# Low parts of the feed-forward weights: from VectorE's subtraction to a negated copy and an adding DMA

## What is computed

```python
for l in range(2):
    hn = rmsnorm(x, g_mix)
    u_a, u_b = split(hn @ w_in)                      # 1024 x 1024
    y_a, h_last = s5_mixer(u_a, h0, ...)             # complex-diagonal scan, GELU, half-GLU
    y_b, hist = pool_mixer(u_b, ...)                 # trailing windows 2, 4, 8, 16
    x = x + concat(y_a, y_b) @ w_out                 # 1024 x 1024
    hf = rmsnorm(x, g_ffn)
    x = x + square(relu(hf @ w_ff1)) @ w_ff2         # 1024 x 4096, 4096 x 1024
return rmsnorm(x, g_final), states, histories
```

## Time and profile before

| | |
|---|---|
| median of 3 runs | 2121.94 us (2121.08 to 2123.07) |
| profiled execution | 2121.07 us, its span 2119.1 us |
| TensorE, matmul | 2063.7 us busy (97%) |
| VectorE | 1070.9 us (51%) |
| ScalarE | 447.7 us (21%) |
| GpSimd | 214.1 us (10%) |
| mean granted clock of TensorE | 0.996 of full speed |
| DMA | 152.77 MB, mean 72 GB/s |

### The profile page before, as it was taken

One profiled execution on the slowest core, in us unless ns is written; L12 is line 12 of the kernel. 1 busy time (PEld: TensorE's weight loads), 2 busy tenths in 40 slices (PEclk: granted clock), 3 DMA queues, 4 the chain that ended last, 5 costly groups with the idle time before them and its releaser, 6 DMA issues.

```text
span 2119.1 us, 29080 instructions
## 1 busy us (share of the span) xinstructions
PE 2063.7 (97%) x12888; PEld 2030.9 (96%) x12888; DVE 1070.9 (51%) x1423; ACT 447.7 (21%) x560; POOL 214.1 (10%) x294
## 2 busy tenths in 40 slices
PE   8999899999999999999999999999999999999997
PEld 7888899999999999999999889999999999999997
DVE  7988464455453535353558725633343434333346
ACT  6232431111010111111332234311111111111112
POOL 2353120000000000010110331100000000000003
PEclk9999999999999999999999999999999999999999
DMA  5455111111211112123242641111111111111112
GB/s 177 135 150 161 53 55 51 46 44 41 92 60 52 60 42 70 42 65 129 95 139 64 196 115 41 40 50 40 50 40 41 50 41 50 41 50 41 45 46 85
DMA packets 62493, 152.77 MB, mean 72 GB/s; under 512 B 8576, under 2 KB 21408, under 8 KB 61984
## 3 DMA queue, kind: packets, MB, share of 16 engines
q1 hardware_dynamic: 49552, 112.76, 17.3%
q0 software_dynamic: 9072, 24.65, 4.2%
q10 hardware_dynamic: 3744, 13.50, 1.6%
HBM read 123.36 MB, written 27.53 MB: 71 GB/s over the span
## 4 chain that ended last, share of the span: by engine, by line
PE 94%; DVE 2%; ACT 2%; issue 1%; DMA 1%; POOL 0%; ACTq 0%; DVEq 0%; POOLq 0%
PE tile L509 89%; PE tile L827 2%; PE small L721 1%; PE small L715 1%; PE small L623 1%; PE small L597 0%; ACT w_high L861 0%; DMA y_a<-ya_dram 0%; DVE pool_s L1210 0%; POOL y_a L1841 0%; DMA ya_dram<-u_blocks 0%; PE small L565 0%; PE small L538 0%; DVE y_a L1665 0%; ACT u_blocks L1095 0%
## 5 line engine op out<-in xcount | busy, mean ns | idle before, releaser
L1548 DVE TENSOR_TENSOR x<-tile,x 128x816 f32<-128x816 f32 (+1 forms) x304 | 205.7, 719 | 490.8 <-PE tile L509 480.9
L509 PE MATMUL tile<-h_high,w_high 128*128 128x408 f32 (+1 forms) x1920 | 426.1, 330 | 10.6 <-DVE w_low L1223 10.6
L509 PE MATMUL tile<-h_low,w_high 128*128 128x408 f32 (+1 forms) x1920 | 422.7, 328 | 0.0
L509 PE MATMUL tile<-h_high,w_low 128*128 128x408 f32 (+1 forms) x1920 | 422.3, 328 | 0.0
L509 PEld LDWEIGHTS tile<-h_high,w_high 128*128 128x128 f32 x1920 | 320.5, 188 | 13.8 <-issue 12.4
L509 PEld LDWEIGHTS tile<-h_low,w_high 128*128 128x128 f32 x1920 | 320.2, 188 | 1.0
L509 PEld LDWEIGHTS tile<-h_high,w_low 128*128 128x128 f32 x1920 | 319.9, 188 | 1.0
L509 PE MATMUL tile<-hidden_high,w_high 128*128 128x408 f32 (+1 forms) x1440 | 317.9, 329 | 0.7
L509 PE MATMUL tile<-hidden_low,w_high 128*128 128x408 f32 (+1 forms) x1440 | 316.4, 328 | 0.0
L509 PE MATMUL tile<-hidden_high,w_low 128*128 128x408 f32 (+1 forms) x1440 | 316.3, 328 | 0.0
L861 ACT ACTIVATE w_high<-w_raw 128x1024 fp32r<-128x1024 f32 x162 | 170.6, 1053 | 664.1 <-PE tile L509 656.7
(11 more groups left out here) (212 smaller groups left out, 1687.0 us busy)
## 6 DMA issues: line engine op xcount, KB each, us to landing
w_raw<-w_blocks SPq DMA_DIRECT2D x164, 512.0 KB, 3.7
x<-x_t ACTq DMA_DIRECT2D x8, 544.0 KB, 10.8
u_blocks<-ua_dram SPq DMA_DIRECT2D x64, 68.0 KB, 2.8
ya_dram<-u_blocks ACTq DMA_DIRECT2D x8, 544.0 KB, 3.5
y_a<-ya_dram POOLq DMA_DIRECT2D x64, 68.0 KB, 2.7
x_kept<-x ACTq DMA_DIRECT2D x8, 544.0 KB, 2.7
cy_dram<-y_quarter POOLq DMA_DIRECT2D x16, 256.0 KB, 2.9
carry_weights<-cy_dram POOLq DMA_DIRECT2D x8, 512.0 KB, 5.2
```

Of the source, the lines that this page charges most:

```text
L509: mm = pe.matmul(ps[tile][:, c, 0:(b - a) * J], lhs, xt[:, k, a * J:b * J], start=(first and n == 0), stop=(last and n == 2))
L1548: ins = v.tensor_tensor(xt, pt_, xt, ALU.add)
```

## The change

For the 128 blocks of the two feed-forwards (`by_adders`), the low part is made in another way. ScalarE writes the high part as before and then, in a second pass over the raw block, minus the high part into the slot of the low part: a copy with scale -1, rounded by its output format as the first one is. GpSimd waits for it and issues a DMA from `raw` to `wlo` that adds to what is there. The 36 blocks of the mixers stay with VectorE. SyncE and TensorE wait for a low part by `low_ready`: for these blocks it is the landing of the DMA, one semaphore for each slot.

```diff
+        def by_adders(b):
+
+            return b < LAYERS * NB and b % NB >= B_FF
+
+        def low_ready(eng, b):
+
+            l, n = divmod(b, NB)
+            if by_adders(b):
+                eng.wait_ge(wlo_added[b % 2], 16 * (l * (NB - B_FF) // 2 + (n - B_FF) // 2 + 1))
+            else:
+                eng.wait_ge(wlo_made, l * B_FF + n + 1)
...
                 if b > 1:
-                    sp.wait_ge(wlo_made, b - 1)
+                    low_ready(sp, b - 2)
...
             def block_at(b):
-                pe.wait_ge(wlo_made, b + 1)
+                low_ready(pe, b)
...
                 act.activation(w_parts(b)[0], raw[:, b % 2, :], ACT.Copy).then_inc(whi_made, 1)
+                if by_adders(b):
+                    act.activation(w_parts(b)[1], raw[:, b % 2, :], ACT.Copy, scale=-1.0).then_inc(wneg_made, 1)
...
             def split_lo(b):
-                if b < LAYERS * NB:
+                if b < LAYERS * NB and not by_adders(b):
...
-            def add_squares(phase):
+            def add_squares(phase, blocks):
+
                 for m in range(1, KD):
...
+                    if m in blocks:
+                        add_low(blocks[m])
+
+            def add_low(b):
+
+                l, n = divmod(b, NB)
+                pool.wait_ge(wneg_made, l * (NB - B_FF) + n - B_FF + 1)
+                pool.dma_start(w_parts(b)[1], raw[:, b % 2, :], accum_op=ALU.add).then_inc(wlo_added[b % 2], 16)
+
+            def add_lows(l, after):
+
+                for n in range(2, 8 * NC - (2, 0)[l]):
+                    add_low(l * NB + B_FF + n)
+                    cc, n = divmod(n, 8)
+                    if l == 0:
+                        after(cc, n)
...
-            add_squares(1)
-            rotations_out()
-            for q in range(4):
-                drive_weights_out(q)
-                carry_weights_out(1, q)
-                kernels_out(1, q)
-            add_squares(2)
+            add_squares(1, {5: B_FF, 7: B_FF + 1})
+
+            def tables_out(cc, n):
+
+                if cc == 2 and n == 7:
+                    rotations_out()
+                if cc in PREP_CHUNKS and n == 5:
+                    drive_weights_out(PREP_CHUNKS[cc])
+                    carry_weights_out(1, PREP_CHUNKS[cc])
+                if cc - 1 in PREP_CHUNKS and n == 0:
+                    kernels_out(1, PREP_CHUNKS[cc - 1])
+            add_lows(0, tables_out)
+            add_squares(2, {1: NB - 2, 3: NB - 1})
...
-            add_squares(3)
+            add_squares(3, {5: NB + B_FF, 7: NB + B_FF + 1})
+            add_lows(1, None)
```

More of the change, by code:

```diff
@@ L255, in hybrid_trunk @@
         wlo_made = sem("wlo_made")
+        wneg_made = sem("wneg_made")
+        wlo_added = [sem(f"wlo_added{i}") for i in range(2)]
         tile_done = sem("tile_done")
```

## The result

| | before | after |
|---|---|---|
| median, same chip | 2122.11 us (2121.08 to 2123.07, 4 runs) | 2142.08 us (2141.02 to 2142.4, 4 runs) |
| profiled span | 2119.1 us | 2139.1 us |
| ratio | | 1.0096, 95% interval 1.0083 to 1.0109 |

The change makes the kernel 20 us slower, where 2143 was forecast. The page of the changed kernel, parts 1, 5 (count, busy us, mean ns, idle before it) and 6 (KB, median us to landing), answers to the earlier trace rows. VectorE's L1223 is now L1239, ScalarE's L861 is L875.

A forecast was written before the change was run, and what follows sets the result against it. TensorE, busy 97% of the span, was taken as the bound, with at most 1.5 us to win. Starts 9.0, half clock 4.8, end 7.5 and turn 0.5 made 21.8; 2121.1 + 21.8 = 2143 us, range 2131 to 2230.

The forecast's parts named there:

- the named places: Where little time is spare: start of each feed-forward, the program's end, the turn to layer 1; 21.8 us together.
- Rival 1: Steady feed-forward chunks stall because the add takes over 7.2 us: 2180 at 8 us, over 2400 at 13; chance 0.28.
- D: Time from when GpSimd's adding DMA may be issued until its data count as landed; taken as 5.5 us.
- Rival 2: Whole program not slower: loss under 4 us if the add lands within 2.6 us, 2124; chance 0.04.
- Rival 3: In layer 0, GpSimd's queue order or a rotations store delays adds at nine places, 2150 to 2161; chance 0.06.
- stops at the two starts, 2 x (D - 1.0): At each feed-forward's third block TensorE waits 4.5 us for the low part, 9.0 together.
- half clock behind them: After each stop at a feed-forward start TensorE runs at 1.2 GHz, losing 2.4 us, 4.8 together.
- the end: Low part of the block before the last two lands late: 6.5 us by data alone, 7.5 with the clock.
- the turn to layer 1: The add shares the engines with a store of x, with 6.1 us of room; 0.5 us lost.
- I keep the slower figure from the rows: Choosing 5.5 us for the add, from a store beside a fetch in the trace, over some 4.1.
- The estimate by the Trainium skill: Add at half a copy's rate, 2.1 us plus 2 us fixed, some 4.1; the sum would be about 12 us.
- 2D - 4.5: Delay of the program's end through the last block's data, fetched only after the preceding add lands; 6.5 us.

The follow-up runs named there:

- e1: Changed kernel with the third feed-forward block of each layer given back to VectorE: 2128.29 us, ratio 1.0035 to the kernel before.
- e2: Changed kernel with the last three blocks of the program given back to VectorE: 2134.39 us, ratio 1.0061 to the kernel before.
- e3: Changed kernel with six blocks back on VectorE (third of each feed-forward, third of layer 0's last chunk, last three): 2121.82 us, 1.0003.
- e7: Kernel before, plus minus passes and DMA adds into an unread buffer for 58 of layer 1's feed-forward blocks: 2121.57 us, 1.0001.
- e4: Changed kernel, TensorE running 21 discarded high-part products before waiting at each layer's third feed-forward block: 2138.73 us, ratio 1.0087.
- e6: Changed kernel with every DMA add done twice, the second issued after the first has landed: 2302.11 us, ratio 1.0845.
- e10: All 128 blocks by DMA add, products needing the low part taken last where TensorE stopped: 2128.8 us, ratio 1.0032.
- e8: Changed kernel, last three blocks on VectorE, low-part products taken last where TensorE stopped and at the very first product: 2120.63 us, 0.9995.
- e5: Changed kernel with GpSimd's DMA copying the raw block over the low part instead of adding: 2134.39 us, ratio 1.0057.

## Why the prediction was right

**Right in mechanism, by experiment.** The loss sits at the named places (e1, e2, e3), the 120 or so adds between them are free (e3, e7), and the clock's share is real (e4). TensorE had waited for VectorE for 1.5 us; taking VectorE's work away could win no more, and the longer way lost wherever less than its length was to spare. Rival 1 (steady stalls) needed D over 7.2 and got 4.4; e6 shows that it exists, with the edge where the prediction put it (7.5 with the hops, against 7.4). Rival 2 (not slower) needed D at 2.6: even a bare copy takes 2.9 and is 13 us slower than before. Rival 3 (GpSimd's order) shows nothing at D = 4.4, but the traffic of layer 1's tables does, with 0.35 us at 1003. Rival 1 was priced too low: for D = 9.3 the prediction has 2230, and e6, whose two adds take 9.3 us from the first issue to the second landing, took 2302. It left out most of the half clock behind so many stops and the longer adds of layer 0.

**Terms of the sum.**

| term | forecast | measured |
|---|---|---|
| D, issue to landing | 5.5 | 4.4, and 0.42 of hops that I left out |
| stops at the two starts, 2 x (D - 1.0) | 9.0 | 3.88 + 3.86 = 7.7 |
| half clock behind them | 4.8 | 2.3 + 1.5 = 3.8 |
| the end | 7.5 | 7.4 |
| the turn to layer 1 | 0.5 | 0.0 |
| other | 0 | 0.6 (layer 0's last chunk), 0.2 |

The step that was off is D: "I keep the slower figure from the rows". I took a plain store beside a fetch for the model, both transfers and all. The estimate by the Trainium skill (Collectives: The Full Stack, the bandwidth ceiling, with DMA: Bandwidth & Descriptors, anatomy of one DMA), 4.1, was nearer to 4.4. With 4.4 my formula gives 6.8 for the two stops; they were 7.7, since I left out the hops to GpSimd and back there, which I had counted in the budget. Two errors of opposite sign; the sum was 1.8 too high. The two starts together moved by 12.0, 0.5 more than their stops and clock. The rest is in the matmuls behind a stop: at full clock in e4 the 216 took 36.01, where the pace of the kernel before gives 35.76, 0.25 us at each start.

Three sums of the prediction are off without effect on its argument. For D = 4 it adds 11 us and writes 2131, where 2121.1 + 11 is 2132. For D = 7.2 its terms give about 2151, not 2155. And SyncE's fetch, by its own rows, starts 1.99 + 5.5 - 2.3 = 5.2 us later than before, not 4.3.

**The end came out by luck, in its size.** The 7.5 of the sum is TensorE's own path, 2078.3 - 2070.8: a restart 5.1 us later and 2.4 us of half clock. Measured were 4.6 and 2.8, two errors that cancel. The path through the last block's data, 2D - 4.5, was the earlier one by 1 us in the forecast (2077.3), and it was the earlier one in the run, by only 0.5 us: TensorE reached the seventh partial tile at 2090.92, and the last add landed 5.5 us after its issue, at 2090.4.

```profile
2084.89 0.86 POOL L1795 DMA_DIRECT2D w_low_last<-w_raw  x1 [8.70 <-ACT w_low_last L877]
...
2090.92 0.35 PE L841 MATMUL tile<-hidden_high,w_high_last 128*128 128x408 f32 x1
```

With D = 4.4 the formula for the data gives 4.3, but the last two adds took 5.7 and 5.5 us, and the fetch between them 4.5; why the last add was slow, with no other transfer beside it, the runs do not show. Without the 2.8 us of half clock TensorE would have waited for it for some 2.3 us (an estimate from these times). In e10, where TensorE stands less before it, the data are late. The clock's delay and the data's are not to be added; whichever is later counts.

## What to carry to other kernels

Moving work off an engine pays by what the bound engine waits for that engine, here 1.5 us of 2119, and costs wherever the new way is longer than the time to spare: look for the few places with the least room (starts of stages, the end), not at the mean. If a longer way is wanted all the same, let the consumer begin with what does not need it, as in e8, or leave those few blocks on the short way, as in e3. Price a stop of TensorE with its half clock too: here 1.3 to 2.8 us behind stops of 2.3 to 6 us, and no half clock behind two of 2.0 and 2.2.

## What the runs showed of the hardware

- An accumulating DMA of 512 KB within the on-chip buffer, issued by GpSimd, lands after 4.4 us, a copy of the same after 2.9. It keeps the DMA engines busy 2.6 us against 1.4, and GpSimd 866 ns against 534. Beside the end of a load of 2 MB one took 7.24 us, and the last one of the program 5.5 with nothing beside it.
- The clock fell after stops of 2.3 us too (e6, e5), not only after the longer one of the earlier trace rows. In e5, after a stop of 2.3 us, it was 0.50 from 326 to 328. It did not fall after every such stop: in e6, after stops of 2.23 us (to 1502.31) and 1.99 us (to 1604.26), it stayed at 1.00.
- It does not always fall while TensorE stands: of the two stops of 3.9 us of the changed kernel, in the first it was at 0.50 before TensorE began again at 324.71, in the second at 1.00 until about 0.6 us after TensorE began again at 1373.55.
- Twenty-one discarded matmul products, 3.5 us, in place of a stop of 3.9 us kept the clock at 1.00 (e4).
